# Latent values split in the closing block and stored as two parts; second unit's high queries and keys requested behind the first row of maxima

## The chip, the cores and the metric

One core of a Trainium2 chip runs the kernel. The metric is device time in microseconds, the median of several runs: 3157.73 us (3157.32 to 3160.18 in 3 runs). A unit, below, is one head of the second attention.

## What is computed

Two transformer layers over 2048 tokens of width 1024, all in fp32: a sliding-window attention with sinks, and a latent attention (MLA). Each is followed by an output projection, a residual, a layer norm and a gated per-layer embedding. The part that matters here:

```python
kv = (_rmsnorm(ckv, kv_norm) @ w_ukv).reshape(B, S, N_HEADS, MLA_NOPE + MLA_V)
k_nope = kv[..., :MLA_NOPE]
v = kv[..., MLA_NOPE:]
...
pr = jax.nn.softmax(jnp.where(kpos[None, :] <= t[:, None], s, NEG_INF), axis=-1)
return jnp.einsum('bhqk,bkhd->bqhd', pr.astype(v.dtype), v)
```

There are 16 heads with 64 values each; the latent `ckv` has 256 columns.

## The kernel before, in words

A product of fp32 numbers is made from parts. Each operand is split into a high part, rounded to the format fp32r, and a low part, what is left; TensorE adds up high x high, high x low and low x high. For one operand, ScalarE makes the high part with a copy and VectorE or POOL makes the low part with a subtraction.

Five phases follow one another, with a barrier between them: the first layer's input projection (`gemm_phase`), its attention (`attention_phase` "swa"), a closing block (`chain_phase` "end0"), the second attention ("mla"), and another closing block ("end1"). All intermediate tensors go through HBM.

**The closing block** (L1039) is a list of tiles [128 x 512] in jobs: "proj", "wo", "pe", and in the first closing block also "in", "uq" and "ukv", each of the last five once per quarter q of the tokens. Every engine walks the same list n = 0, 1, ... in order. TensorE writes tile n to one of four banks (`tile`). ScalarE and VectorE clear the bank one place later (`evict`, L1569 and L1703), SP stores the tile at n + 2 (`store`, L1353, `store_due`). A job "ukv" has 16 tiles of 6 products: eight of kind "split", the keys (kn), for which ScalarE writes the high part to `out_f` (L1592), VectorE the low part to `out_l` (L1727), and SP stores 256 KB twice (L1359, L1360); and then eight of kind "v", the values: 128 tokens x 8 heads x 64, in fp32, which VectorE alone copies to `out_f` (L1732) and SP stores as 256 KB (L1370). `out_f` has six places (`n_out`) that all kinds but "turn" take in turn, and `wait_out_free` (L1258) waits until the tile six places before is stored. ScalarE also issues the weight loads and rounds the weights (L1529), POOL makes the low parts of the weights of these jobs (L1953). `raw` is two sets of eight slices [128 x 512] that receive the input of the jobs in turn; the input of a job "ukv" fills the first two slices. Four tiles before its end, SP requests the second attention's first high queries and keys (`first_loads`).

**The second attention** (L1991) walks 16 units of 40 steps; a step is a block of 128 keys against up to 512 queries. Per step TensorE makes the scores in three passes (`scored`), and three steps later two products with the values (`weigh`): the stationary operand is `vals` [128 keys x 128], 64 columns of high values beside 64 of low ones. ScalarE takes the exponential twice (L2379 rounded, L2380 not), POOL subtracts for the low part (L2529), VectorE adds up the denominators (L2458). Beside steps 0 to 32 of unit u, TensorE makes the row maxima of unit u + 1 (`item`) from the high queries and keys, in two banks, and VectorE reduces them (L2403). When a unit's maxima are done they are transposed, negated (L2433), and ScalarE sends the row by DMA into the query tile (`max_row`, L2312): it is one more row of the product that makes the scores.

SP loads: `load_high(u)` (L2160) is five DMAs of high queries and keys, `load_low(u)` (L2166) is five DMAs of low ones and one of the values. The values of unit u arrive unsplit in `v_raw` [128 x 16 x 64], 512 KB; at step 20 of the unit before, ScalarE rounds them into `vals` (`values_high`, L2328), and at step 21 VectorE subtracts (`values_low`, L2437). For unit 0 both happen before the first step: on ScalarE ahead of `max_row(0)`, on VectorE behind `negate(0)`.

SP's order at the start is `load_low(0)`, `load_high(1)`, a wait for the first row of maxima, `load_high(2)`, `load_low(1)`. Step 0 of a unit waits for the low loads and its row of maxima. Only 12 of the first unit's 40 maxima (`lead`) are made ahead of its first score, the others in its steps 0 to 7, and those of unit 1 begin at step 10.

Of the kernel before, what the change touches and what calls it, by code (L numbers as in the profile page):

```python
# [16 lines left out]
F32 = mybir.dt.float32  # L17
# [4 lines left out]
P = 128  # L22
# [1016 lines left out]
def chain_phase(nc, consts, name, cfg):  # L1039
# [23 lines left out]
    with ExitStack() as ctx:  # L1063
# [62 lines left out]
        outs, olds, turns = upto("pe"), upto("wo", "pe"), upto("pe", "z")  # L1126
        highs, rotated = upto("split"), upto("turn", "kr")

# [7 lines left out]

        out_tiles = [n for n, x in enumerate(tiles) if x["kind"] != "turn"]
        place, stored_at, filled_upto = {}, {}, [0] * n_out
# [4 lines left out]
        user_before = {n: out_tiles[m - n_out] for m, n in enumerate(out_tiles) if m >= n_out}  # L1143
        turn_tiles = [n for n, x in enumerate(tiles) if x["kind"] == "turn"]


# [53 lines left out]
        if latent:  # L1200
# [28 lines left out]
             "turn_hi", "rot_ok"))  # L1229
        turn_stored = [s.sem(f"turn_stored{b}") for b in range(2)]  # L1230
        block = ctx.enter_context(nc.Block())

# [34 lines left out]
        def wait_w_lo(eng, b):  # L1267
            if b < n_dve_blocks:
                eng.wait_ge(w_lo_ok, b + 1)
            else:  # L1270
                eng.wait_ge(w_lo_p_ok, b - n_dve_blocks + 1)

        def wait_old_in(eng, n):
# [29 lines left out]
        def _(sp):  # L1303
# [49 lines left out]
            def store(n):  # L1353
                x = tiles[n]
                kind, q = x["kind"], x["q"]
                wait_ready(sp, n)
                if kind == "split":
                    dst = latent["q_nope"] if jobs[x["job"]][0] == "uq" else latent["k_nope"]
                    sp.dma_start(dst[0][x["i"], :, tok(q)], out_f[place[n]][:]).then_inc(stored[place[n]], 16)  # L1359
                    sp.dma_start(dst[1][x["i"], :, tok(q)], out_l[place[n]]).then_inc(stored[place[n]], 16)  # L1360
                elif kind == "turn":
                    for part in range(2):
                        sp.dma_start(latent["q_rope"][part][x["at"], x["i"] - 1, :, tok(q)],
                                     turn_out[2 * x["at"] + part][:]).then_inc(turn_stored[x["at"]], 16)
                elif kind == "kr":
                    for part in range(2):
                        sp.dma_start(latent["k_rope"][part][:, tok(q)],
                                     out_f[place[n]][part * ROPE:(part + 1) * ROPE, :]).then_inc(stored[place[n]], 16)
                elif kind == "v":
                    sp.dma_start(latent["v"][x["i"], :, 4 * q + x["at"], :], out_f[place[n]][:]  # L1370
                                 ).then_inc(stored[place[n]], 16)
                else:
                    if kind == "z":
                        dst, r = latent["z"], x["i"] - len(latent["rows"])
                    else:
                        dst = {"proj": cfg["proj"], "wo": cfg["summed"], "pe": cfg["dst"],
                               "lat": latent and latent["c"]}[kind]
                        r = x["i"]
                    sp.dma_start(dst.rearrange("(r p) t -> r p t", p=P)[r, :, tok(q)], out_f[place[n]][:]
                                 ).then_inc(stored[place[n]], 16)  # L1380
# [51 lines left out]
            if latent:  # L1432
                sp.wait_ge(tab_stored, 32 * NTC)
                for b in range(2):
                    sp.wait_ge(turn_stored[b], 16 * len(turn_tiles))

        @block.tensor
# [59 lines left out]
        def _(act):  # L1497
# [71 lines left out]
            def evict(n):  # L1569
# [11 lines left out]
                elif x["kind"] == "pe":  # L1581
                    act.wait_ge(product, n + 1)
                    act.activation(bank, bank, ACT.Sigmoid).then_inc(sig_ok, 1)
                elif x["kind"] == "z":
                    act.wait_ge(product, n + 1)
                    if tiles[n - 2]["kind"] == "z":
                        act.wait_ge(dve_out, by_dve[n - 2])
                    act.activation(sig[n % 2][:], bank, ACT.Sigmoid).then_inc(sig_ok, 1)
                elif x["kind"] == "split":
                    act.wait_ge(product, n + 1)  # L1590
                    wait_out_free(act, n)
                    act.copy(out_f[place[n]][:].bitcast(F32R), bank).then_inc(hi_ok, 1)  # L1592
                elif x["kind"] == "kr":
                    act.wait_ge(product, n + 1)
                    act.wait_ge(rms_ok, x["q"] + 1)
                    act.copy(key_b[0:ROPE, :], bank[ROPE:2 * ROPE, :]).then_inc(key_moved, 1)
# [84 lines left out]
        def _(dve):  # L1681
# [21 lines left out]
            def evict(n):  # L1703
# [25 lines left out]
                elif x["kind"] == "v":  # L1729
                    dve.wait_ge(product, n + 1)  # L1730
                    wait_out_free(dve, n)
                    vec.tensor_copy(out_f[place[n]][:], bank).then_inc(dve_out, 1)  # L1732
                elif x["kind"] == "turn" and x["at"] == 1:
# [257 lines left out]
def attention_phase(nc, consts, name, cfg):  # L1991
# [20 lines left out]
    with ExitStack() as ctx:  # L2012
# [18 lines left out]
        vals = [s.sb(f"v{b}", [P, vb, P if long else 2 * P], F32R) for b in range(2)]  # L2031
        if long:
            v_raw = [s.sb(f"v_raw{b}", [P, vb, HEAD_DIM]) for b in range(2)]
            v_hi_ok, v_lo_ok = s.sem("v_hi_ok"), s.sem("v_lo_ok")
        prob = [s.sb(f"p{b}", [P, TC]) for b in range(nbuf)]
# [118 lines left out]

        values_at, copy_at = 20, 5
        tail = store_lag + 1

        @block.sync
        def _(sp):
# [6 lines left out]
            def load_low(u):  # L2166
# [9 lines left out]
                if u >= 2:  # L2176
                    sp.wait_ge(scores, ends[u - 2])
                v_tile = v_raw[u % 2] if long else vals[u % 2]
                for n, (dst, src) in enumerate(cfg["load_b"](u, q_tiles[1][u % 2], k_tiles[1][u % 2], v_tile)):
                    if n == cfg["n_load_b"] - 1 and u >= 2:  # L2180
                        if long:
                            sp.wait_ge(v_lo_ok, u - 1)
                        else:
                            sp.wait_ge(weighed, ends[u - 2])
                    sp.dma_start(dst.bitcast(F32), src).then_inc(ld_b[u % 2], 16)
# [3 lines left out]
            load_low(0)  # L2189
            load_high(1)  # L2190
            for c in range(len(chunks)):
                u = chunks[c][0]
                if c == 0 or chunks[c - 1][0] != u:
                    if c == 0:
                        sp.wait_ge(mrow[0], 16)
                    if u + 2 < units:
                        load_high(u + 2)
# [10 lines left out]
        def _(pe):  # L2208
# [57 lines left out]
            def weigh(g):  # L2266
                u, k, st = flat[g]
                c, off = chunk_of[g], st["off"]
                pe.wait_ge(probs, g + 1)
                if long and k == 0:  # L2270
                    pe.wait_ge(v_lo_ok, u + 1)
                if st["first"] and c >= 2:
# [34 lines left out]
        def _(act):  # L2307
# [15 lines left out]

            def values_high(u):
                act.wait_ge(ld_b[u % 2], 16 * cfg["n_load_b"] * (u // 2 + 1))
                if u >= 2:
                    act.wait_ge(weighed, ends[u - 2])
                act.copy(vals[u % 2][:, :, 0:HEAD_DIM], v_raw[u % 2][:]).then_inc(v_hi_ok, 1)  # L2328

            def low_half(c):  # L2330
# [29 lines left out]
            for c in range(ahead + 1):  # L2360
                load_gate(c)
            if long:
                values_high(0)
            max_row(0)
            for g in range(total + tail):
                if g < total:
                    u, k, st = flat[g]
                    if long and k == values_at and u + 1 < units:
                        values_high(u + 1)
                    off, b, c = st["off"], g % nbuf, chunk_of[g]  # L2370
# [24 lines left out]
        def _(dve):  # L2395
# [38 lines left out]

            def values_low(u):
                dve.wait_ge(v_hi_ok, u + 1)
                vec.tensor_tensor(vals[u % 2][:, :, HEAD_DIM:P], v_raw[u % 2][:],  # L2437
                                  vals[u % 2][:, :, 0:HEAD_DIM].bitcast(F32), ALU.subtract).then_inc(v_lo_ok, 1)

            def add(g):  # L2440
# [45 lines left out]
            negate(0)  # L2486
            if long:
                values_low(0)
            else:
                copy_queries(0)  # L2490
            for g in range(total + tail):
                if g < total:
                    u, k, st = flat[g]
                    if long and k == values_at + 1 and u + 1 < units:
                        values_low(u + 1)
                    if not long and k == copy_at and u + 1 < units:
# [108 lines left out]
def mla_config(q_nope, q_rope, k_nope, k_rope, v, gates, out, dens, next_loads, here):  # L2605
# [32 lines left out]
    def load_b(u, q_tile, k_tile, vals):  # L2638
        yield from load(u, q_tile, k_tile, 1)
        half_heads = HEADS // 2  # L2640
        yield vals[:], v[u // half_heads].rearrange("p n (h d) -> h p n d", d=HEAD_DIM)[u % half_heads]

# [20 lines left out]
def build(nc, a, out):  # L2663
# [3 lines left out]
    with ctx:  # L2667
# [68 lines left out]
        qn, qr = parts("qn", [HEADS // 2, P, SEQ]), parts("qr", [2, 2, P, SEQ])  # L2736
        kr, kn, v1 = parts("kr", [ROPE, SEQ]), parts("kn", [HEADS // 2, P, SEQ]), dram("v1", [2, P, NB, HEADS // 2 * HEAD_DIM])
        mla = mla_config(qn, qr, kn, kr, v1, z1, o1, den1, loads1, here)
# [89 lines left out]
```

## Time and profile before

| | |
|---|---|
| median of 3 runs | 3157.73 us |
| the profiled execution's own time | 3165.66 us |
| its span | 3163.8 us |
| TensorE (PE) busy | 2972.4 us |
| closing block's last four jobs ("ukv") | some 1603 to 1697 us |
| first product of the second attention | 1709.5 us |
| its first score | 1730.5 us |
| one unit | 61.5 us |

The span is the profiled one, from first to last instruction. PE is TensorE, DVE VectorE, ACT ScalarE, POOL GpSimd, SP the engine that issues most DMAs; a "q" behind a name is its sequencer. "end_" tiles belong to a closing block, "mla_" ones to the second attention, "early_" ones are shared by both. PEclk is the clock granted to TensorE as a share of 2.4 GHz. L2210 is a helper through which all products of the attention go. The mean time of a product includes overlap with the next.

### The profile page before, as it was taken

How to read it: one execution, taken by the hardware profiler on the slowest of the kernel's cores; microseconds unless marked ns; L12 is line 12 of the kernel's file. 1: busy time of each engine (PE TensorE's matmuls, PEld its weight loads, DVE VectorE, ACT ScalarE, POOL GpSimd, SP SyncE). 2: the span in 40 equal slices, each digit the busy share in tenths (PEclk: the TensorE clock that was granted, in tenths of full speed). 3: DMA queues.
4: the chain of work that ended last, by engine and by line, in shares of the span. 5: the costliest groups of instructions: out<-in, count | busy, mean ns of one | idle time of the engine just before them, and what ended most of it. 6: DMA issues, size and time to landing. Idle time of an engine off the chain costs nothing. (4 is left out here: it accounts for less than half of the span.)

```text
span 3163.8 us, 41025 instructions
## 1 busy us (share of the span) xinstructions
PE 2972.4 (94%) x13537; PEld 2336.3 (74%) x13537; DVE 1937.6 (61%) x2712; ACT 1623.4 (51%) x2814; POOL 1457.6 (46%) x1163
## 2 busy tenths in 40 slices
PE   8999988998999999999996999999999999899998
PEld 6888876666887787778774677777777777588876
DVE  3543215552588755555653777777777777357875
ACT  3111114666346444444542576777677677544553
POOL 0022104664233530001752688888788788523353
PEclk9999998999999999999997899999999999999999
DMA  5343447665986765555999243343234323399674
GB/s 159 88 133 116 115 140 213 197 206 170 294 275 209 241 222 173 172 157 171 346 369 263 46 103 64 63 97 82 62 75 103 64 63 93 99 299 283 221 238 144
DMA packets 294279, 524.36 MB, mean 166 GB/s; under 512 B 62720, under 2 KB 117632, under 8 KB 286912
## 3 DMA queue, kind: packets, MB, share of 16 engines
q1 hardware_dynamic: 219840, 374.45, 40.8%
q10 hardware_dynamic: 74240, 147.49, 15.3%
q8 instruction: 97, 1.59, 0.2%
q14 instruction: 102, 0.84, 0.1%
HBM read 349.47 MB, written 172.10 MB: 165 GB/s over the span
## 5 line engine op out<-in xcount | busy, mean ns | idle before, releaser
L2529 POOL TENSOR_TENSOR mla_pl<-mla_p,mla_ph 128x512 fp32r<-128x512 f32 (+3 forms) x640 | 718.7, 1140 | 214.1 <-ACT mla_p L2380 207.8
L1460 PE MATMUL end_bank<-end_xh,end_whi 128*128 128x512 f32 x1808 | 717.8, 397 | 46.2 <-DVE end_wlo L1686 17.5
L1461 PE MATMUL end_bank<-end_xl,end_whi 128*128 128x512 f32 x1808 | 709.0, 392 | 0.0
L1462 PE MATMUL end_bank<-end_xh,end_wlo 128*128 128x512 f32 x1808 | 708.9, 392 | 0.0
L1529 ACT CAST end_whi<-early_wraw 128x1024 fp32r<-128x1024 f32 (+1 forms) x228 | 234.0, 1026 | 593.4 <-PE end_bank L1462 526.2
L2379 ACT ACTIVATE mla_ph<-mla_score 128x512 fp32r<-128x512 f32 (+3 forms) x640 | 340.4, 532 | 291.2 <-PE mla_score L2210 287.5
L1686 DVE TENSOR_TENSOR end_wlo<-early_wraw,end_whi 128x1024 fp32r<-128x1024 f32 x188 | 255.4, 1359 | 322.7 <-ACT end_whi L1529 322.6
L2403 DVE TENSOR_REDUCE mla_mx<-mla_mx 128x1 f32<-128x512 f32 (+3 forms) x640 | 371.5, 603 | 125.0 <-PE mla_mx L2210 124.2
L1460 PEld LDWEIGHTS end_bank<-end_xh,end_whi 128*128 128x128 f32 x1808 | 342.6, 189 | 134.5 <-issue 25.8
L2458 DVE TENSOR_TENSOR mla_acc<-mla_acc,mla_p 128x512 f32<-128x512 f32 (+3 forms) x576 | 348.7, 605 | 123.4 <-ACT mla_p L2380 119.6
L1461 PEld LDWEIGHTS end_bank<-end_xl,end_whi 128*128 128x128 f32 x1808 | 342.6, 190 | 73.2 <-issue 2.9
L1462 PEld LDWEIGHTS end_bank<-end_xh,end_wlo 128*128 128x128 f32 x1808 | 342.5, 189 | 72.5
L2210 PE MATMUL mla_score<-mla_q,mla_k 96*128 96x512 f32 (+7 forms) x1200 | 353.8, 397 | 0.0
L2380 ACT ACTIVATE mla_p<-mla_score 128x512 f32<-128x512 f32 (+3 forms) x640 | 337.2, 527 | 0.0
L2210 PEld LDWEIGHTS mla_score<-mla_q,mla_k 96*128 96x128 f32 (+1 forms) x1200 | 229.7, 195 | 55.3 <-issue 19.2
L2210 PE MATMUL mla_o<-mla_ph,mla_v 128*128 128x512 f32 (+3 forms) x640 | 250.7, 392 | 7.1 <-ACT mla_den_row L2344 7.1
L2210 PE MATMUL mla_o<-mla_pl,mla_v 128*128 128x512 f32 (+3 forms) x640 | 239.5, 374 | 1.7 <-POOL mla_pl L2529 1.5
L904 PE MATMUL in_bank<-in_xh,in_whi 128*128 128x512 f32 x576 | 226.5, 393 | 15.2 <-DVE in_xl L737 15.2
L908 PE MATMUL in_bank<-in_xh,in_wlo 128*128 128x512 f32 x576 | 225.7, 392 | 0.0
L906 PE MATMUL in_bank<-in_xl,in_whi 128*128 128x512 f32 x576 | 225.6, 392 | 0.0
L2529 POOL TENSOR_TENSOR swa_pl<-swa_p,swa_ph 128x512 fp32r<-128x512 f32 x124 | 165.3, 1343 | 104.1 <-ACT swa_p L2380 102.9
L2210 PE MATMUL mla_mx<-mla_k,mla_q 96*128 96x512 f32 (+3 forms) x400 | 141.1, 389 | 24.0 <-DVE mla_mx L2403 23.9
(234 smaller groups left out, 4981.9 us busy)
## 6 DMA issues: line engine op xcount, KB each, us to landing
early_wraw<-in_pe_gate ACTq DMA_DIRECT2D x64, 512.0 KB, 5.3
early_wraw<-in_w_out ACTq DMA_DIRECT2D x62, 512.0 KB, 7.9
early_wraw<-in_w_in ACTq DMA_DIRECT2D x56, 512.0 KB, 3.7
scratch_q<-in_rope SPq DMA_DIRECT2D x64, 256.0 KB, 2.9
swa_q<-scratch_q SPq DMA_DIRECT2D x8, 2048.0 KB, 9.4
end_factor<-scratch_inv SPq DMA_DIRECT2D x64, 256.0 KB, 10.0
scratch_proj<-end_out_f SPq DMA_DIRECT2D x64, 256.0 KB, 6.9
scratch_sum<-end_out_f SPq DMA_DIRECT2D x64, 256.0 KB, 6.5
```

Of the source, the lines that this page charges most:

```text
L904: nc.tensor.matmul(banks[b][t][:], w_hi[b][:, at], hi[b][:, k, tok], start=(k == 0), stop=False)
L1460: nc.tensor.matmul(bank, wh[:, at], xh[:, k0 + k, :], start=(k == 0), stop=False)
L1461: nc.tensor.matmul(bank, wh[:, at], xl[:, k0 + k, :], start=False, stop=False)
L1462: last = nc.tensor.matmul(bank, wl[:, at], xh[:, k0 + k, :], start=False, stop=(k == kc - 1))
L1529: act.copy(w_hi[b % n_w][:, 0:width], w_raw[b % n_raw][:, 0:width]).then_inc(w_hi_ok, 1)
L1686: vec.tensor_tensor(w_lo[b % n_w][:], w_raw[b % n_raw][:], w_hi[b % n_w][:].bitcast(F32), ALU.subtract).then_inc(w_lo_ok, 1)
L2210: return nc.tensor.matmul(out, lhs, rhs, start=start, stop=stop)
L2379: act.activation(p_hi[b][:, off:TC], bank[:, off:TC], ACT.Exp, scale=scale)
L2380: act.activation(prob[b][:, off:TC], bank[:, off:TC], ACT.Exp, scale=scale).then_inc(probs, 1)
L2403: vec.tensor_reduce(mx[:].rearrange("p (j n) -> p j n", j=x["groups"])[:, :, x["col"]], src, AX.X, ALU.max).then_inc(mx_done, 1)
L2458: vec.tensor_tensor(into[:, both], acc_ps[:, both], now[:, both], ALU.add).then_inc(summed, 1)
L2529: pool.tensor_tensor(p_lo[b][:, off:TC], prob[b][:, off:TC], p_hi[b][:, off:TC].bitcast(F32), ALU.subtract).then_inc(p_lo_ok, 1)
```

## The change

In the closing block the value tiles are evicted as two parts: ScalarE writes the rounded high part from the bank, VectorE subtracts it from the bank for the low part. Both go, head by head side by side (64 high, 64 low), to one of three places of 4 KB a partition in slices 2 to 7 of the job's own `raw` set, and SP stores 512 KB in one DMA. Value tiles no longer take places of `out_f`. The HBM tensor `v1` is twice as wide. In the attention the values load straight into `vals`; `v_raw`, `values_high`, `values_low` and their semaphores are gone, and the load's last DMA waits for the last weighted sum of the unit two before. In the second attention `load_high(1)` is issued behind the wait for the first row of maxima.

```diff
@@ chain_phase
-        highs, rotated = upto("split"), upto("turn", "kr")
+        highs, rotated, values = upto("split", "v"), upto("turn", "kr"), upto("v")
...
-        out_tiles = [n for n, x in enumerate(tiles) if x["kind"] != "turn"]
+        out_tiles = [n for n, x in enumerate(tiles) if x["kind"] not in ("turn", "v")]
...
+        v_tiles = [n for n, x in enumerate(tiles) if x["kind"] == "v"]
...
+        v_stored = [s.sem(f"v_stored{b}") for b in range(3)]
...
+        def v_tile(n):
+            m = (values[n] - 1) % 3
+            return raw[tiles[n]["job"] % 2][:, 2 + 2 * m:4 + 2 * m, :].rearrange(
+                "p a t -> p (a t)").rearrange("p (h two d) -> p h two d", two=2, d=HEAD_DIM)
+
+        def wait_v_free(eng, n):
+            m = values[n] - 1
+            eng.wait_ge(x_lo, pieces_upto[tiles[n]["job"] - 2])
+            if m >= 3:
+                wait_v_stored(eng, v_tiles[m - 3])
+
+        def wait_v_stored(eng, n):
+            eng.wait_ge(v_stored[values[n] % 3], 16 * ((values[n] - 1) // 3 + 1))
...
                 elif kind == "v":
-                    sp.dma_start(latent["v"][x["i"], :, 4 * q + x["at"], :], out_f[place[n]][:]
-                                 ).then_inc(stored[place[n]], 16)
+                    sp.dma_start(latent["v"][x["i"], :, 4 * q + x["at"], :], v_tile(n).rearrange(
+                        "p h two d -> p (h two d)")).then_inc(v_stored[values[n] % 3], 16)
...
+                for b in range(3):
+                    sp.wait_ge(v_stored[b], 16 * sum(values[n] % 3 == b for n in v_tiles))
@@ chain_phase, ScalarE's evict
+                elif x["kind"] == "v":
+                    act.wait_ge(product, n + 1)
+                    wait_v_free(act, n)
+                    act.copy(v_tile(n)[:, :, 0, :].bitcast(F32R), bank.rearrange("p (h d) -> p h d", d=HEAD_DIM)
+                             ).then_inc(hi_ok, 1)
@@ chain_phase, VectorE's evict
                 elif x["kind"] == "v":
-                    dve.wait_ge(product, n + 1)
-                    wait_out_free(dve, n)
-                    vec.tensor_copy(out_f[place[n]][:], bank).then_inc(dve_out, 1)
+                    dve.wait_ge(hi_ok, highs[n])
+                    vec.tensor_tensor(v_tile(n)[:, :, 1, :].bitcast(F32R), bank.rearrange("p (h d) -> p h d", d=HEAD_DIM),
+                                      v_tile(n)[:, :, 0, :], ALU.subtract).then_inc(dve_out, 1)
@@ attention_phase
-        if long:
-            v_raw = [s.sb(f"v_raw{b}", [P, vb, HEAD_DIM]) for b in range(2)]
-            v_hi_ok, v_lo_ok = s.sem("v_hi_ok"), s.sem("v_lo_ok")
...
-                v_tile = v_raw[u % 2] if long else vals[u % 2]
-                for n, (dst, src) in enumerate(cfg["load_b"](u, q_tiles[1][u % 2], k_tiles[1][u % 2], v_tile)):
+                for n, (dst, src) in enumerate(cfg["load_b"](u, q_tiles[1][u % 2], k_tiles[1][u % 2], vals[u % 2])):
                     if n == cfg["n_load_b"] - 1 and u >= 2:
-                        if long:
-                            sp.wait_ge(v_lo_ok, u - 1)
-                        else:
-                            sp.wait_ge(weighed, ends[u - 2])
+                        sp.wait_ge(weighed, ends[u - 2])
...
             load_low(0)
-            load_high(1)
+            if not lead:
+                load_high(1)
...
                     if c == 0:
                         sp.wait_ge(mrow[0], 16)
+                        if lead:
+                            load_high(1)
...
-                if long and k == 0:
-                    pe.wait_ge(v_lo_ok, u + 1)
...
-            def values_high(u):
-                act.wait_ge(ld_b[u % 2], 16 * cfg["n_load_b"] * (u // 2 + 1))
-                if u >= 2:
-                    act.wait_ge(weighed, ends[u - 2])
-                act.copy(vals[u % 2][:, :, 0:HEAD_DIM], v_raw[u % 2][:]).then_inc(v_hi_ok, 1)
...
-            if long:
-                values_high(0)
             max_row(0)
...
-                    if long and k == values_at and u + 1 < units:
-                        values_high(u + 1)
...
-            def values_low(u):
-                dve.wait_ge(v_hi_ok, u + 1)
-                vec.tensor_tensor(vals[u % 2][:, :, HEAD_DIM:P], v_raw[u % 2][:],
-                                  vals[u % 2][:, :, 0:HEAD_DIM].bitcast(F32), ALU.subtract).then_inc(v_lo_ok, 1)
...
-            if long:
-                values_low(0)
-            else:
+            if not long:
                 copy_queries(0)
...
-                    if long and k == values_at + 1 and u + 1 < units:
-                        values_low(u + 1)
@@ mla_config, build
-        yield vals[:], v[u // half_heads].rearrange("p n (h d) -> h p n d", d=HEAD_DIM)[u % half_heads]
+        yield vals[:], v[u // half_heads].rearrange("p n (h d) -> h p n d", d=P)[u % half_heads]
...
-        kr, kn, v1 = ..., dram("v1", [2, P, NB, HEADS // 2 * HEAD_DIM])
+        kr, kn, v1 = ..., dram("v1", [2, P, NB, HEADS // 2 * P])
```

## Rows read from the trace of the kernel before

**Rows 1.** the page: busy us and share of the span
```profile
PE 2972.4 (94%) x13537; PEld 2336.3 (74%) x13537; DVE 1937.6 (61%) x2712; ACT 1623.4 (51%) x2814; POOL 1457.6 (46%) x1163
```
**Rows 2.** windows by stage, closing block to attention; the header names the columns
```profile
core 0: us, PE busy (x) PEld busy (x) DVE busy (x) ACT busy (x) POOL busy (x), PEclk, DMA share, GB/s
1502.00:1604.00 102.00, 96.15 (x408) 76.83 (x407) 67.76 (x85) 59.07 (x93) 77.61 (x48) 0.98 0.99 354
...
1643.00:1666.00 23.00, 21.97 (x96) 17.94 (x96) 10.85 (x18) 11.16 (x16) 12.09 (x6) 1.00 1.05 368
1666.00:1696.00 30.00, 27.34 (x120) 22.18 (x120) 15.45 (x23) 8.60 (x12) 9.60 (x4) 1.00 1.00 346
1696.00:1710.00 14.00, 1.08 (x6) 0.69 (x4) 1.61 (x3) 0.00 (x0) 0.00 (x0) 0.70 0.81 213
1710.00:1730.00 20.00, 7.45 (x20) 3.96 (x19) 8.09 (x16) 2.33 (x2) 5.29 (x3) 0.50 0.97 192
```
**Rows 3.** DMA, 1604 to 1696 us
```profile
DMA packets 19432, 32.90 MB, mean 358 GB/s; under 512 B 1863, under 2 KB 4935, under 8 KB 19426
```
**Rows 4.** groups, 1604:1696 us (busy, mean ns | idle before, whose)
```profile
L1732 DVE COPY end_out_f<-end_bank 128x512 f32<-128x512 f32 x30 | 20.1, 689 | 18.9 <-DMA scratch_kn_lo<-end_factor 9.0 <-DMA scratch_kn_lo<-end_sig 3.9 <-DMA scratch_v<-end_out_f 3.2
L1592 ACT CAST end_out_f<-end_bank 128x512 fp32r<-128x512 f32 x29 | 16.7, 585 | 18.8 <-DMA scratch_kn_lo<-end_sig 6.6 <-DMA scratch_v<-end_out_f 5.0 <-PE end_bank L1462 4.0
...
L1727 DVE TENSOR_TENSOR end_factor<-end_bank,end_out_f 128x512 fp32r<-128x512 f32 x20 | 13.5, 689 | 12.3 <-ACT end_out_f L1592 12.3
```
**Rows 5.** line 1370, the stores of the values
```profile
DMA to landing us min/median/max: 2.8/6.6/9.4
```
**Rows 6.** windows, unit 1 of the attention; columns as in rows 2
```profile
1815.80:1877.30 61.50, 58.59 (x284) 44.35 (x283) 47.73 (x87) 44.28 (x94) 49.90 (x45) 0.97 0.37 78
```
**Rows 7.** waits of PE, 1820:2720 us, then 1765:1820 us
```profile
PE mla_mx L2210 <- DVE mla_mx L2403: 33.9, 41, 1.8
PE mla_o L2210 <- ACT mla_den_row L2344: 7.1, 15, 0.7
...
PE mla_mx L2210 <- DVE mla_mx L2403: 2.3, 4, 0.9
```
**Rows 8.** timeline of unit 1: start, us, instruction, idle before
```profile
1844.54 1.03 ACT L2328 CAST mla_v<-mla_v_raw 128x1024 fp32r<-128x1024 f32 x1
...
1847.17 1.80 DVE L2437 TENSOR_TENSOR mla_v<-mla_v_raw,mla_v 128x1024 fp32r<-128x1024 f32 x1
...
1848.90 1.27 DVE L2403 TENSOR_REDUCE mla_mx<-mla_mx 128x1 f32<-128x512 f32 x2
...
1849.63 0.33 PE L2210 MATMUL mla_mx<-mla_k,mla_q 96*128 96x128 f32 x1 [1.83 <-DVE mla_mx L2403]
...
1850.23 0.50 PE L2210 MATMUL mla_mx<-mla_k,mla_q 96*128 96x512 f32 x1 [0.20 <-DVE mla_mx L2403]
```
**Rows 9.** windows, first and last half-clock stretch of units 1 to 14
```profile
1851.84:1855.25 3.41, 3.41 (x10) 2.34 (x9) 1.86 (x4) 1.66 (x4) 1.28 (x1) 0.50 0.12 41
2650.55:2653.97 3.42, 3.42 (x10) 2.35 (x10) 2.35 (x4) 1.08 (x2) 1.22 (x2) 0.50 0.11 38
```
**Rows 10.** timeline of the attention's start
```profile
1719.49 0.28 DVE L2433 TENSOR_SCALAR mla_m_t<-mla_mx 8x128 fp32r<-8x128 f32 x1 [0.47 <-PE mla_mx L2238]
...
1723.98 1.04 ACT L2328 CAST mla_v<-mla_v_raw 128x1024 fp32r<-128x1024 f32 x1 [36.64 <-DMA mla_v_raw<-scratch_v]
1723.99 0.75 ACTq L2312 DMA_DIRECT2D early_q<-mla_m_t  x1
...
1730.46 0.76 PE L2210 MATMUL mla_score<-early_q,early_k 97*128 97x512 f32 x1 [11.00 <-DMA early_q<-mla_m_t]
```
**Rows 11.** tile mla_v, who writes it
```profile
L2328 ACT CAST mla_v<-mla_v_raw x16: 1030/1032/1044, 1724.0 to 2643.9; 128x1024 fp32r<-128x1024 f32 x16
L2437 DVE TENSOR_TENSOR mla_v<-mla_v_raw,mla_v x16: 1224/1804/1808, 1725.1 to 2646.5; 128x1024 fp32r<-128x1024 f32 x16
```
**Rows 12.** line 2312, the rows of maxima
```profile
DMA to landing us min/median/max: 1.8/2.0/3.9
```

More of the change, by code:

```diff
@@ L2153, in turns_at @@
             return out
-        values_at, copy_at = 20, 5
+        copy_at = 5
         tail = store_lag + 1
@@ L2736, in build @@
         qn, qr = parts("qn", [HEADS // 2, P, SEQ]), parts("qr", [2, 2, P, SEQ])
-        kr, kn, v1 = parts("kr", [ROPE, SEQ]), parts("kn", [HEADS // 2, P, SEQ]), dram("v1", [2, P, NB, HEADS // 2 * HEAD_DIM])
+        kr, kn, v1 = parts("kr", [ROPE, SEQ]), parts("kn", [HEADS // 2, P, SEQ]), dram("v1", [2, P, NB, HEADS // 2 * P])
         mla = mla_config(qn, qr, kn, kr, v1, z1, o1, den1, loads1, here)
```

## The prediction

> **What bounds the kernel now.** The page comes first: TensorE is busy for 94% of the span, VectorE, the next of the engines that compute, for 61% [rows 1]. Time is therefore to be had where TensorE idles or runs at half clock, or where a stretch is bound by something else. The change touches two places, so I read each with its own view.
>
> In the closing block's last stages, the windows by stage show a DMA share of 0.99 to 1.05 from 1502 us to 1696 us, while TensorE is busy for 21.97 of 23 us or less [rows 2]. The 16 DMA engines have no time left there: 32.90 MB go out in 92 us, 358 GB/s [rows 3]. One job of 16 tiles takes 23.0 us, 1.44 us a tile. The evictions wait for stores to land: VectorE's copies of the values stood idle 18.9 us, ScalarE's high halves 18.8 us, mostly for landings [rows 4]. So this stage goes by bytes.
>
> In the second unit's attention, one unit takes 61.5 us with TensorE busy for 58.6 us [rows 6]. Nearly all of its idle time there is its wait for the row maxima, 33.9 us in 41 waits, the longest 1.8 us [rows 7]. The timeline of unit 1 shows where the longest sits [rows 8]: ScalarE rounds a head's values at 1844.54 (1.03 us), the exponentials behind it come late, VectorE starts the low half at 1847.17 (1.80 us), its next maxima come only at 1848.90, and TensorE, which has two banks for them, stands 1.83 us and then 0.20 us more. Two microseconds on, the granted clock falls: 0.50 from 1851.84 to 1855.25 us, the lower of its two levels, 1.2 GHz [rows 9]. The last such stretch is at 2650.55 us; there are 14, one in each of units 1 to 14, each within 3 us behind this wait, and they make the unit's mean 0.97 [rows 6].
>
> Between the stages TensorE waits too: it has nothing from 1719.46 to 1730.46 us, 11.00 us for the row of maxima [rows 10].
>
> **The change, part by part, against the profiled execution (3165.7 us, 7.9 us over the median of 3157.7).**
>
> *Values split once, in the closing block.* ScalarE gets 32 high halves at 0.585 us, 4.7 us per job of 23 us, and is busy for about 11 of 23 us now [rows 2, 4]: covered. VectorE's 32 copies (0.689 us) become 32 subtractions (0.689 us for the same shape) [rows 4]: nothing. If that cover went, the four banks would stay full and TensorE would wait for up to 0.6 us a tile, 19 us over 32 tiles. Each store grows from 256 to 512 KB: 32 x 262,144 bytes = 8.39 MB more in a stretch without DMA time to spare. At 358 GB/s that is 23.4 us [rows 3]. The two bounds: pieces of 4 KB instead of 2 KB a partition may cost less per byte, and the drain behind 1696 us runs at a share of 0.81 [rows 2], so that perhaps half is paid, 12 us; and the values now have three places instead of a share of six. A slot's round is 0.59 + 0.69 us of eviction, some 0.3 us of issue and the landing. With the shortest landing seen, 2.8 us [rows 5], and 0.7 us for the second half of the bytes, three places allow a tile per 1.7 us, slower than the 1.44 us of now but close to the 524 KB that DMA needs anyway; with ScalarE waiting for a slot, its weight roundings queue behind it and POOL's low halves of the weights behind those. That could make it 35 us. I take 24 us, the row's rate and little for the slots.
>
> The Trainium skill ("DMA: Bandwidth & Descriptors", Specifications) puts the HBM limit of one core at about 358 GB/s, which speaks against storing the values twice as wide; the trace agrees (358 GB/s). Had the fabric ceiling of 435 GB/s on the same page applied, the term would be 19 us.
>
> *No split in the attention.* It removes 16 roundings (1.03 us) and 16 subtractions (1.22 to 1.80 us) [rows 11]. What they cost is what they hold up. Units 1 to 14: 1.83 + 0.20 = 2.03 us of TensorE idle, and the half-clock stretch of 3.41 us, in which TensorE is busy throughout and does half the work: 1.7 us [rows 8, 9]. That is 3.73 x 14 = 52.2 us. In unit 0, the four waits for maxima sum to 2.3 us [rows 7] and no clock falls behind them: 2 us. Unit 15 has no split beside it. What is late next? Without these the unit would be 57.8 us; VectorE then has 47.7 - 1.8 = 45.9 us to do, POOL 49.9 us, ScalarE 43.3 us [rows 6], so TensorE remains the bound with 8 us to spare. Bounds: only the idle time comes back (30.4 us), or all of the 54.2 us; I take the latter since the only other TensorE wait in a unit is about 0.5 us for a row of denominators [rows 7].
>
> *The load of the values* takes 1 MB a head instead of 0.5 MB, in pieces of 512 instead of 256 bytes. In the attention the DMA share is 0.37 [rows 6], and the load has a whole unit: nothing. Its last piece now waits for the last weighted sum of two units ago instead of for the low half. SP alone waits there, about three steps, and behind it is only the next unit's load, 55 us before its use: nothing. Without the cover it would be those three steps, some 4.5 us a unit.
>
> *The start.* Now ScalarE rounds the first values before it may issue the row of maxima. They land at 1723.98, the row is issued then, behind the second unit's high queries and keys, and is there at 1730.3; yet the row was ready for issue at 1719.8 [rows 10]. Afterwards ScalarE issues it at 1719.8, with only the low loads ahead. The first score needs these and the row. The low loads land at 1724.0 plus at most a microsecond for the larger values; the row, between 1.8 us (the least landing of such a row in the trace [rows 12]) and 6.3 us (from this one's issue to the first score) behind its issue, at 1721.6 to 1726.1. So TensorE resumes at 1724.5 to 1726.1 instead of 1730.46: 4.4 to 6 us, I take 5.5. The five moved loads (1.5 MB, 8 us at 190 GB/s [rows 2]) go out at about 1724 and are there by 1735; unit 1's maxima begin at step 10 of unit 0, over 30 us behind the first score. Covered; without the cover, up to 8 us once. Two further loads queue behind them on SP, for which nobody waits before unit 1.
>
> **Sum:** +24 - 52.2 - 2 - 5.5 = -35.7 us, 3130 us for such an execution, **3122 us** against the median.
>
> **The rivals.**
>
> *A: the clock does not follow.* TensorE's idle time goes, but the half-clock stretches stay, because smaller waits remain. For: the wait of 0.5 us for the denominators stays. Against: each stretch stands right behind the 1.83 us wait and nowhere else in the units. It gives 14 x 1.7 = 24 us less: 3146 us.
>
> *B: the wider stores are paid dearer.* At 35 to 45 us: 3133 to 3143 us. For it: three places, and ScalarE's queue behind them. Against: the kn stores ahead keep six places and so keep DMA busy.
>
> *C: they are nearly hidden.* 12 us or less: 3110 us or below. Against it: DMA shares of 1.00 to 1.05.
>
> *D, the other side: three places starve the closing block.* A value tile then takes (1.6 us + landing) / 3. At the longest landing seen for half the bytes, 9.4 us [rows 5], with 0.7 us more, that is 3.9 us instead of 1.44 us, 79 us over 32 tiles, and the kernel ends at 3157.7 + 79 - 59.7 = 3177 us. It decides from a landing of about 8 us on, where 32 x ((1.6 + 8.3)/3 - 1.44) meets the 59.7 us won. For: the median now is 6.6 us. Against: that is mostly the queue of six places of kn, and only three value stores can stand in front of each other.
>
> *E: the change does nothing in the attention*, since the maxima are late for another reason. Then +24 - 5.5: 3176 us. Against: 14 pairs of 2.03 us behind the split are 28.4 of the 33.9 us of such waits.
>
> **How the numbers follow.** My forecast 0.64, A 0.09, B 0.12, C 0.07, D 0.05, E 0.03. The likeliest case's own range is 3110 to 3132. The range of 8 in 10 reaches to B and into A and to the edge of C: 3104 to 3143. A measurement of this kernel tells about 0.2%, 6.3 us, from no change. Faster by more: all but D, E and the worst of A with B together, 0.89; slower: 0.07; same: 0.04.
>
> **What would show it.** In the changed profile: units of 57.8 us with TensorE waits for maxima below 0.5 us and a granted clock of 1.00 over a unit; DMA share still about 1.0 in the closing block with jobs of 28 to 29 us; value stores that land within 6 us; the first score about 15 us behind the first product of the attention (21 us now). Units of 59.5 us would speak for A, jobs over 31 us or landings of 8 us for B or D, units of 61.5 us for E.

## The result, and the profile after

The changed kernel takes 3118.4 us (median of 4 runs, 3114.1 to 3120.5), the kernel before, run beside it, 3158.95 us: a ratio of 0.9867, 95% interval 0.985 to 0.9884. That is 40.6 us off; the forecast was 3122 us. The profiled execution of the changed kernel takes 3119.7 us against 3165.7 us. Of these 46 us, 7.5 lie ahead of anything that the change touches: the first store of kn starts at 1603.18 us before and at 1595.63 us after. That is a difference between executions and not between kernels: in e2 and e5, below, the kernel before reaches this store at 1595.0 and 1594.9 us, and in e4 the changed one at 1603.1 us.

First the closing block. The windows view of the kernel before, from that store to the attention's first product; columns as in [rows 2]:

```profile
1603.20:1709.50 106.30, 85.16 (x361) 67.98 (x360) 45.63 (x67) 38.01 (x55) 41.05 (x20) 0.95 1.01 340
```

The same stretch and one unit of the attention in the changed kernel:

```profile
1595.60:1727.60 132.00, 92.22 (x360) 68.54 (x359) 44.73 (x67) 54.67 (x87) 40.98 (x20) 0.91 0.97 339
...
1826.40:1884.00 57.60, 56.71 (x284) 43.37 (x283) 45.94 (x86) 43.52 (x93) 49.05 (x45) 1.00 0.43 92
```

The closing block's stretch grew by 25.7 us, and the DMA share in it fell from 1.01 to 0.97. TensorE's busy time grew with it, from 85.16 to 92.22 us for the same products, at a mean clock of 0.91 instead of 0.95; no run tells how much of the 25.7 us that is. A unit went from 61.5 us at a mean clock of 0.97 [rows 6] to 57.6 us at 1.00. The waits of TensorE in units 1 to 15 of the changed kernel (1826 to 2700 us), us in total, count, longest:

```profile
PE mla_o L2230 <- ACT mla_den_row L2356: 7.2, 15, 0.7
PE mla_mx L2230 <- DVE mla_mx L2411: 6.1, 14, 0.6
```

The second line had 33.9 us in 41 waits before [rows 7]: the long wait is gone. How long the units are can be read off the rows of maxima, one DMA a unit; the first of the mla_q ones is unit 1's, the last of the early_q ones unit 15's. "First and last start" of these issues, kernel before:

```profile
L2312 ACTq DMA_DIRECT2D mla_q<-mla_m_t x10: 568/568/589, 1810.6 to 2610.0; - x10
L2312 ACTq DMA_DIRECT2D early_q<-mla_m_t x7: 568/569/751, 1724.0 to 2671.4; - x7
```

and changed kernel:

```profile
L2330 ACTq DMA_DIRECT2D mla_q<-mla_m_t x10: 569/569/585, 1821.2 to 2570.2; - x10
L2330 ACTq DMA_DIRECT2D early_q<-mla_m_t x7: 569/569/752, 1738.0 to 2627.8; - x7
```

2671.4 - 1810.6 = 860.8 us for 14 units, 2627.8 - 1821.2 = 806.6 us after: 54.2 us less, 3.87 us a unit.

Waits in the changed kernel's closing block, 1604 to 1720 us. Two are ScalarE's for a place of the value tiles, two TensorE's for the bank behind them:

```profile
ACT early_raw L1615 <- DMA scratch_v<-early_raw: 16.2, 7, 8.0
ACT end_raw L1615 <- DMA scratch_v<-end_raw: 14.5, 8, 5.3
...
PE end_bank L1474 <- DVE end_raw L1755: 11.1, 4, 3.5
...
PE end_bank L1474 <- DVE early_raw L1755: 8.3, 3, 4.3
```

ScalarE waits 30.7 us for a value store to land, and TensorE 19.4 us for the eviction behind it. Over the whole stretch ScalarE's waits of this kind sum to 39.1 us. The landings of these stores, twice as large as in [rows 5]:

```profile
DMA to landing us min/median/max: 2.6/7.0/9.3
```

The attention's start, timeline of the changed kernel. It answers to [rows 10]:

```profile
1727.64 0.44 PE L2230 MATMUL mla_mx<-early_k,early_q 96*128 96x128 f32 x1 [12.29 <-PEq L1063]
...
1737.97 0.75 ACTq L2330 DMA_DIRECT2D early_q<-mla_m_t  x1
...
1742.26 0.77 PE L2230 MATMUL mla_score<-early_q,early_k 97*128 97x512 f32 x1 [4.64 <-DMA early_q<-mla_m_t]
```

The row goes out 10.3 us behind the first product (14.5 us before), and the first score starts at 14.6 us (21.0 us before), 4.3 us behind the row's issue.

| term | forecast | measured |
|---|---|---|
| closing block's stretch | +24 | +25.7 |
| attention's start | -5.5 | -6.4 |
| unit 0 | -2 | -1.2 |
| units 1 to 14 | -52.2 | -54.2 |
| sum | -35.7 | -36.1 |

What is left, some 2 us behind the last row of maxima and the 7.5 us ahead of the change, is not explained by it. Against the medians the sum is 4 us short.

### The profile page after: what moved, and what is told of

Same layout as the page of the kernel before. It is cut to its first block and busy times, and to the rows that moved or that the text cites. A ratio compares the mean times of both kernels' runs of the same rounds, so it can differ in the third digit from the quotient of the medians.

```text
span 3117.8 us, 41010 instructions
## 1 busy us (share of the span) xinstructions
PE 2946.5 (95%) x13537; PEld 2317.2 (74%) x13537; DVE 1909.3 (61%) x2696; ACT 1628.0 (52%) x2830; POOL 1450.3 (47%) x1163
## 5 line engine op out<-in xcount | busy, mean ns | idle before, releaser
L2528 POOL TENSOR_TENSOR mla_pl<-mla_p,mla_ph 128x512 fp32r<-128x512 f32 (+3 forms) x640 | 707.3, 1120 | 164.0 <-ACT mla_p L2388 156.4
L2230 PE MATMUL mla_score<-mla_q,mla_k 96*128 96x512 f32 (+7 forms) x1200 | 345.0, 390 | 0.0
L1977 POOL TENSOR_TENSOR end_wlo<-early_wraw,end_whi 128x768 fp32r<-128x768 f32 (+1 forms) x40 | 84.7, 2117 | 162.7 <-ACT end_whi L1548 162.6
```

Source lines behind the costliest of these rows:

```text
L2230: return nc.tensor.matmul(out, lhs, rhs, start=start, stop=stop)
L2528: pool.tensor_tensor(p_lo[b][:, off:TC], prob[b][:, off:TC], p_hi[b][:, off:TC].bitcast(F32), ALU.subtract).then_inc(p_lo_ok, 1)
```

## The experiments

Each is told with the theory it was to test. "The stretch" is that from the first store of kn to the attention's first product, and a time "behind the first product" is counted from the latter.

**The subtraction elsewhere (e2_low36).** The kernel before, with all its work and its closing block:

```diff
-                    if long and k == values_at + 1 and u + 1 < units:
+                    if long and k == 36 and u + 1 < units:
                         values_low(u + 1)
```

> The kernel before with only VectorE's subtraction for the next unit's values moved from step 21 to step 36 of a unit, where no row maxima are made any more; same work, no change in the closing block. My theory: the split cost the attention what it did because it stood among the maxima. Then the wait of 1.83 us and the half-clock stretches go although all the work stays: units of 57.6 to 57.8 us, 54 to 58 us off the time, about 3101 us, which is faster than the changed kernel. Rival: the work itself costs (1.0 us of ScalarE and 1.8 us of VectorE a unit), wherever it stands: units of 60 to 61.5 us, 3140 to 3158 us.

It takes 3114.7 us, a ratio of 0.9862 (0.9837 to 0.9888). One unit, and TensorE's waits for maxima from 1830 to 2670 us:

```profile
1820.00:1878.30 58.30, 57.24 (x284) 43.32 (x283) 47.56 (x88) 44.23 (x94) 49.80 (x45) 1.00 0.40 84
```

```profile
PE mla_mx L2210 <- DVE mla_mx L2403: 7.1, 27, 0.4
```

VectorE is as busy as before (47.6 us), yet the unit is 3.2 us shorter, its clock is 1.00 and the long wait is gone. So it was the place of the subtraction among the maxima that cost, not its 1.8 us. This one changed number gets what the whole change gets. The expectation was 0.6 us a unit too good: 58.3 and not 57.6 us.

**In two halves (e3_halves).** The subtraction stays among the maxima, half of it at step 21 and half at step 29 (`values_low` takes the half as a second argument; that part is left out here):

```diff
...
-                    if long and k == values_at + 1 and u + 1 < units:
-                        values_low(u + 1)
+                    if long and k in (values_at + 1, values_at + 9) and u + 1 < units:
+                        values_low(u + 1, 0 if k == values_at + 1 else 1)
```

> The kernel before with VectorE's subtraction for the next unit's values in two halves, at steps 21 and 29, still among the maxima. It tells the idle time from the clock. My theory: each half (0.9 us) leaves TensorE at most about 1.1 us of wait, and the granted clock stays at 1.00 over the unit as behind the waits of 1.6 us and less elsewhere: units of 58.5 to 59.5 us, 28 to 42 us off the time. Rival: the half-clock stretches come once a unit whatever the wait is: mean clock 0.97 in a unit and units of 60.3 us or more.

One run, 3150.1 us, where 28 to 42 us off were expected. My expectation failed on the clock. The wait shrank to 1.30 us (timeline of units 1 and 3):

```profile
1846.35 0.33 PE L2210 MATMUL mla_mx<-mla_k,mla_q 96*128 96x128 f32 x1 [1.30 <-DVE mla_mx L2403]
...
1968.37 0.33 PE L2210 MATMUL mla_mx<-mla_k,mla_q 96*128 96x128 f32 x1 [1.30 <-DVE mla_mx L2403]
```

but a half-clock stretch followed in 11 of the 14 units all the same. The windows of units 1 and 3:

```profile
1811.50:1872.50 61.00, 58.62 (x284) 44.33 (x283) 47.76 (x88) 44.19 (x94) 49.68 (x45) 0.97 0.38 79
1933.50:1993.00 59.50, 57.12 (x284) 43.34 (x283) 47.68 (x88) 44.23 (x94) 49.74 (x45) 1.00 0.38 80
```

The same wait, once with the stretch and once without: it is worth 61.0 - 59.5 = 1.5 us, against 1.7 us in the forecast. The rival, a stretch every unit whatever the wait, falls too: units 3, 7 and 11 have none, and in e2 no unit from 1 to 14 has one. By their rows of maxima (1807.9 to 2657.1 us) the 14 units take 849.2 us, 11.6 us less than before.

**The move of the loads alone (e1_move).** The kernel before with `load_high(1)` behind the wait for the first row:

> The kernel before with one part of the change alone: the second unit's high queries and keys are requested behind the first row of maxima. My theory: the row is still issued at about 14.5 us behind the attention's first product (ScalarE rounds the first values ahead of it), but no 1.5 MB of loads stand in front of it, so it lands in 2 to 3 us instead of 6.3 us; first score 17 to 18 us behind the first product instead of 21.0 us, 3 to 4 us off the time (3155 us). Rival: the row is slow because of its own path and not because of the loads; then 21 us and no change. The units stay at 61.5 us.

3154.9 us in 10 runs, a ratio of 0.998 (0.997 to 0.9991): a gain of about 5 us that clears the noise narrowly. Timeline:

```profile
1706.79 0.45 PE L2213 MATMUL mla_mx<-early_k,early_q 96*128 96x128 f32 x1 [11.70 <-PEq L1063]
...
1719.75 0.75 ACTq L2315 DMA_DIRECT2D early_q<-mla_m_t  x1
...
1721.75 0.76 PE L2213 MATMUL mla_score<-early_q,early_k 97*128 97x512 f32 x1 [4.98 <-DMA early_q<-mla_m_t]
```

The row needs 2.0 us instead of 6.5 us once nothing stands in the queues with it, and the low loads, too, land 1.5 us sooner: the first score comes 15.0 us behind the first product, sooner than the 17 to 18 us expected. The move alone gives 6.0 us of the 6.4 us.

**The change without the move (e4_after_nomove).** The same edit undone in the changed kernel:

> The changed kernel with the loads of the second unit's high queries and keys back in their old place, ahead of the first row of maxima. My theory: ScalarE issues the row at once when it is ready, 10.3 us behind the first product, but 1.5 MB stand in the queues with it: first score 16 to 19 us behind the first product instead of 14.6 us, 2 to 4 us slower than the changed kernel (3121 us). Rival: the move does nothing when the row is issued early, and the first score stays at 14.6 us.

3125.1 us, a ratio of 0.9887 (0.9862 to 0.9911) to the kernel before. In its timeline the row goes out 10.3 us behind the first product, as in the changed kernel, and the first score starts at 17.3 us:

```profile
1733.88 0.45 PE L2227 MATMUL mla_mx<-early_k,early_q 96*128 96x128 f32 x1 [12.18 <-PEq L1063]
...
1744.21 0.75 ACTq L2327 DMA_DIRECT2D early_q<-mla_m_t  x1
...
1751.19 0.77 PE L2227 MATMUL mla_score<-early_q,early_k 97*128 97x512 f32 x1 [7.33 <-DMA early_q<-mla_m_t]
```

So the early issue alone gives 3.7 us, the move alone 6.0 us, both 6.4 us: they mostly remove the same wait. By the medians this run is 6.7 us slower than the changed kernel, more than the 2.7 us that the timeline shows; the rest is not explained.

**Half of each value tile stored (e6_half_store).** In the changed kernel:

```diff
-                    sp.dma_start(latent["v"][x["i"], :, 4 * q + x["at"], :], v_tile(n).rearrange(
+                    sp.dma_start(latent["v"][x["i"], :, 4 * q + x["at"], 0:TC], v_tile(n)[:, 0:4].rearrange(
                         "p h two d -> p (h two d)")).then_inc(v_stored[values[n] % 3], 16)
...
-        yield vals[:], v[u // half_heads].rearrange("p n (h d) -> h p n d", d=P)[u % half_heads]
+        yield vals[:], v[u // half_heads].rearrange("p n (h d) -> h p n d", d=P)[u % half_heads % 4]
```

> The changed kernel in which each value tile is still split in two parts in three places, but only the half of it that holds four of its eight heads is stored (256 KB instead of 512 KB); heads 4 to 7 of each eight are left out, and the attention reads heads 0 to 3 in their stead. It tells bytes from places. My theory, bytes: 8.39 MB less, and the stretch from the first store of kn to the attention's first product falls from 132.0 us to 107 to 111 us. Rival, places: the three places and ScalarE's waits for them cost it, and it stays above 120 us.

One run, 3109.9 us; half of the values are left out of it. The windows row of its stretch, and ScalarE's waits for a place:

```profile
1596.10:1718.00 121.90, 90.37 (x360) 71.08 (x361) 45.27 (x67) 55.24 (x87) 41.00 (x20) 0.90 0.91 297
```

```profile
ACT early_raw L1615 <- DMA scratch_v<-early_raw: 18.8, 4, 8.6
ACT end_raw L1615 <- DMA scratch_v<-end_raw: 12.1, 4, 4.8
```

With as few bytes as before the change, the stretch is 121.9 us and not 107 to 111. The bytes account for 10.1 us only; 15.6 us remain, the DMA share has fallen to 0.91, and ScalarE still waits 30.9 us for a place. My theory of bytes fails here.

**Two places (e7_two_places).** `% 3` becomes `% 2` in the changed kernel, and a tile waits for the store of the one two before:

> The changed kernel with two places for value tiles instead of three. If bytes alone set the closing block, DMA stays full and it costs under 4 us. If the round of a place counts (1.6 us of eviction and issue, 3.5 us for an unhindered landing), a value tile takes 2.55 us instead of 1.7 us, and the stretch of 132.0 us grows by 8 to 16 us. My theory of the forecast says the latter here, and that three places are just about enough.

One run, 3136.0 us:

```profile
1601.10:1743.30 142.20, 98.13 (x360) 72.47 (x358) 45.03 (x67) 54.68 (x87) 40.99 (x20) 0.86 0.89 315
```

The stretch is 10.2 us longer, inside the 8 to 16 us expected from the round of a place, while the DMA share falls to 0.89.

**Six places (e9_six_places).** The other set of `raw` is free in slices 2 to 7 as well:

```diff
-            m = (values[n] - 1) % 3
-            return raw[tiles[n]["job"] % 2][:, 2 + 2 * m:4 + 2 * m, :].rearrange(
+            m = (values[n] - 1) % 6
+            return raw[m // 3][:, 2 + 2 * (m % 3):4 + 2 * (m % 3), :].rearrange(
...
-            eng.wait_ge(x_lo, pieces_upto[tiles[n]["job"] - 2])
-            if m >= 3:
-                wait_v_stored(eng, v_tiles[m - 3])
+            eng.wait_ge(x_lo, pieces_upto[tiles[n]["job"] - 1])
+            if m >= 6:
+                wait_v_stored(eng, v_tiles[m - 6])
...
```

> The changed kernel with six places for the value tiles (three in each of the two sets of the input) instead of three, bytes unchanged. In the changed kernel DMA was busy for 0.97 of the stretch of 132.0 us between the first store of kn and the attention's first product, that is 128 us of work against 107 us before; with half the bytes stored 0.91 of 121.9 us, with two places 0.89 of 142.3 us. Theory now: bytes set a floor, places add to it. With six places the DMA share returns to 1.01 or more and the stretch to 122 to 127 us: 5 to 10 us faster than the changed kernel, 3108 to 3113 us. Rival one, bytes hardly matter (the half store gave back only 10 of 25.7 us): then it falls under 118 us. Rival two, places do not matter at three: 131 to 133 us.

3104.4 us, a ratio of 0.9825 (0.9807 to 0.9843) to the kernel before, 14 us faster than the changed kernel by the medians.

```profile
1595.70:1712.00 116.30, 87.05 (x361) 67.43 (x360) 44.78 (x67) 54.00 (x87) 41.05 (x20) 0.93 1.03 384
```

Its first 101 us, without the drain behind the last products, to set beside the 92 us of [rows 3], and ScalarE's waits for a place in the whole stretch:

```profile
1596.00:1697.00 101.00, 86.74 (x359) 67.14 (x358) 43.14 (x65) 53.11 (x86) 41.05 (x20) 0.98 1.05 397
```

```profile
ACT early_raw L1615 <- DMA scratch_v<-early_raw: 4.3, 3, 2.0
...
ACT end_raw L1615 <- DMA scratch_v<-end_raw: 2.2, 1, 2.2
```

The stretch is 116.3 us: the places give back 15.7 us, more than the 5 to 10 us expected, and 10.0 us are left over the kernel before. It even falls under the 118 us of my first rival, by which bytes hardly matter. ScalarE's waits for a place fell from 39.1 to 6.5 us. The two experiments agree. Halving the bytes at three places gives back 10.1 us and leaves 15.6 us; widening to six places with all the bytes gives back 15.7 us and leaves 10.0 us. The evictions' added steps are in both remainders, so if the parts simply add, these steps cost nothing that can be seen. All this holds to a microsecond or two: where the closing block is untouched, the stretch is 105.7 to 107.6 us (e5, e1), and in e4, where it is the changed kernel's, 130.8 us. And the rows show why the reckoning in bytes went wrong: 384 GB/s over the stretch, where the kernel before had 340 GB/s at a DMA share of 1.01, and 397 GB/s without the drain, against 358 GB/s.

**The first loads later (e10_loads_later).** `n == total - 4` becomes `n == total - 1` for `first_loads` in the changed kernel, since its last two value tiles wait 7.7 us for a place behind those loads:

> The changed kernel with the attention's first high loads requested behind the store of the third last value tile instead of behind the sixth last. In the changed kernel the last two value tiles wait 7.7 us for a place, since the stores that hold it stand behind those loads. If that tail costs, the stretch of 132.0 us shortens by 1 to 4 us. Rival: DMA works through the same bytes either way and the stretch stays within 1 us, or grows where the later loads land later.

3122.1 us, a ratio of 0.9884 (0.9864 to 0.9905); the stretch is 132.4 us:

```profile
1595.50:1727.90 132.40, 92.08 (x360) 70.83 (x358) 45.44 (x67) 55.26 (x87) 40.97 (x20) 0.90 0.96 338
```

The stretch did not shorten, as the rival had it: the long wait at the end costs nothing by itself.

**The two cheap edits together (e5_low36_start).** The kernel before with the subtraction at step 36, the move, and `max_row(0)` ahead of `values_high(0)`:

> The kernel before with the subtraction at step 36, the second unit's high loads behind the first row of maxima, and ScalarE issuing that row ahead of its rounding of the first values. No change in the closing block, where the stretch from the first store of kn to the attention's first product should stay at 106 to 107 us (132.0 us in the changed kernel). Units of 58.3 us as with the subtraction moved alone; first score 13 to 15 us behind the first product. Together some 50 us off: 3108 to 3112 us, 7 to 10 us faster than the changed kernel. Rival: the gains of the two edits overlap, and it stays at 3115 us.

3106.9 us, a ratio of 0.9828 (0.9809 to 0.9847), a microsecond under the expected range. The first score starts 13.6 us behind the first product, one microsecond sooner than in the changed kernel. The gains add.

**And the rounding at step 30 (e8_high30_low36):**

```diff
-                    if long and k == values_at and u + 1 < units:
+                    if long and k == 30 and u + 1 < units:
                         values_high(u + 1)
```

> The same kernel with ScalarE's rounding of the next unit's values at step 30 instead of step 20 as well. At step 30 TensorE takes 2.1 us and ScalarE works 1.1 us of it, so the 1.03 us fit. If the 0.7 us by which a unit with the subtraction moved (58.3 us) is longer than one of the changed kernel (57.6 us) is the rounding's delay at step 20, units come to 57.6 to 57.8 us: 8 to 10 us less again, 3099 to 3103 us. Rival: the 0.7 us belong to the subtraction at step 36 or to the work itself, and units stay at 58.2 us or more.

3097.4 us (3094.5 to 3100.4), a ratio of 0.9792 (0.9773 to 0.9812). The windows of one unit and of the closing block's stretch:

```profile
1815.80:1873.40 57.60, 56.78 (x282) 43.20 (x281) 47.43 (x88) 44.47 (x93) 49.80 (x45) 1.00 0.39 83
...
1595.30:1702.10 106.80, 85.77 (x360) 67.85 (x360) 45.66 (x67) 38.07 (x55) 41.05 (x20) 0.94 0.99 338
```

Units come to 57.7 us by their rows of maxima, with all the work of the split in them, so the 0.6 us of e2 were the rounding's place at step 20. The closing block keeps its 106.8 us. This is the fastest version run: it beats the kernel before by 63 us (ratio 0.9792, where the changed kernel has 0.9867), by moving four things and adding none.

## Why the prediction was right, point by point

**The attention** came out as forecast, in mechanism and size: 54.2 us against 52.2. The timeline's chain of [rows 8] is shown by e2: take the subtraction away from the maxima and the wait and the half-clock stretches go, with the work still there. The parts can now be set side by side, per unit: 0.6 us for the rounding at step 20 (e2 against e8), 1.5 us for a half-clock stretch (e3), and the rest, 61.5 - 57.7 - 0.6 - 1.5 = 1.7 us, for the subtraction's idle time. The forecast had 2.03 us for the idle time and 1.7 us for the clock, 3.73 us together against 3.8 us; it had no term for the rounding, and that the rounding's 0.6 us was in part inside its 2.03 us is my reading, not shown. What remained the bound was TensorE, as argued from [rows 6].

**Rival A** (the clock does not follow) falls: 1.00 over a unit. **Rival E** falls: the waits were the split's.

**The start** was right in size (6.4 against 5.5 us), and its mechanism holds: the row is issued 10.3 us behind the first product, and the 4.3 us from its issue to the first score lie inside the forecast's bounds of 1.8 and 6.3 us. What it did not tell apart is its two parts. The step "the row was ready for issue at 1719.8" is true, but the early issue alone gives 3.7 us (e4) and the move of the loads alone 6.0 of the 6.4 us (e1), because both edits remove mostly one and the same wait. The loads ahead of the row were the bigger part: from the row's issue to the first score it took 6.5 us with them and 2.0 us without.

**The closing block** was right in size (25.7 against 24 us) by luck: two errors cancel. The step that failed is "in a stretch without DMA time to spare. At 358 GB/s that is 23.4 us". It read a DMA share of 1.0 as a full pipe (the 32.90 MB that it has "go out" are loads too, the weights above all). With the places widened the same engines carry 384 GB/s (e9), and the bytes cost 10 us. The other step, "I take 24 us, the row's rate and little for the slots", had put under 1 us on the three places, which cost 15.7 us. The sentence on the round of a place (a tile per 1.7 us) was the better argument; the expectation of e7, built on it, had 8 to 16 us, and 10.2 us came. The forecast gave it too little weight, since "the kn stores ahead keep six places and so keep DMA busy" sounded like a cover. They do not cover it: value tiles come eight in a row, and ScalarE stands still for 39.1 us over the stretch (6.5 us in e9). The forecast's own signs told of it, too: its value stores were to land within 6 us and took 7.0 us at the median, and jobs over 31 us were to speak for the rivals with dear stores or too few places. By the first store of kn of each job, a job takes 32.0 us in the changed kernel. By the same measure it took 25.5 us before, where the forecast started from 23.0 us, one window of the trace. The limit of about 358 GB/s that the Trainium skill ("DMA: Bandwidth & Descriptors", Specifications) gives for one core, with which the forecast said the trace agrees, is not what bound it: e9 moves 384 GB/s over 116 us, and the measurement decides.

**Rival D** had the mechanism (places) and not the price: stores of the doubled size land in 7.0 us at the median, under the 8 us from which it would have decided. **Rival B** named the right cause, the three places and ScalarE's queue behind them, at 9 us or more above what came, and **C** nearly the right price of the bytes.

**The load of the values** was covered, as forecast: the share of DMA in a unit rose from 0.37 [rows 6] to 0.43, and TensorE waits for no load there.

What stays open: how the clock is granted behind a wait of 1.30 us, in 11 units of 14 and not in the others, was not told apart; whether the 10 us of e9 are bytes alone, since that the parts add is assumed; and what the half-clock time of TensorE in the closing block costs (mean clock 0.91 against 0.95 before).

## What to carry to other kernels

Ask where an instruction stands before asking what it costs: here 1.8 us of VectorE moved by 15 steps gave what shifting the whole work to another phase gave, and the phase that took the work paid 26 us for it. When a store grows and gets fewer places, reckon the round of a place (eviction, issue, landing) and not only the bytes; and do not read a DMA share of 1 as the end of its throughput, since the GB/s beside it may still rise. When two edits end the same wait, try each alone before counting both.

## What the runs showed of the hardware

A TensorE wait of 1.83 us was followed by a half-clock stretch in all of 14 units [rows 8, 9], one of 1.30 us in 11 of 14, and one stretch cost 1.5 us of a unit (61.0 against 59.5 us). A DMA of 4 KB (the row of maxima, eight rows) took 2.0 us from issue to use with the loads ahead of it landed (e1), 4.3 us with the low loads requested some 6 to 10 us before it (the changed kernel), and 6.5 us with 1.5 MB more requested on another queue just before it (the kernel before). DMA with a busy share of 1.01 moved 340 GB/s in the kernel before and, at 1.03, 384 GB/s in e9, whose value stores write 4 KB per partition instead of 2 KB.
